# A ninth expert pair in a once-used buffer of its own, and GpSimd's transfers issued by SyncE

## What is computed

```python
n = rms_norm(h, g_mix)
proj = n @ w_in                       # z, xbc, dt, q, k, v, two gates
y_ssd = ssd_mixer(z, xbc, dt, ...) @ w_ssd_out
y_sb = stick_breaking_attention(q, k, v) @ w_sb_out
h = h + (gates[0] * y_ssd + gates[1] * y_sb) @ w_out
h = h + memory_cross_attention(rms_norm(h, g_xattn), rms_norm(mem, g_mem), w_xq, w_xkv, w_xo)
h = h + moe_ffn(rms_norm(h, g_moe), w_router, b_router, w_gu, b_gu, w_down, b_down)
return rms_norm(h, g_final)
```

## Time and profile before

| what | us |
|---|---|
| median of 3 runs | 1315.87 (1315.59 to 1319.79) |
| profiled execution, its own time | 1318.25 |
| its span in the profile | 1316.4 |
| PE busy | 1221.2 (93%) |
| DVE, ACT, POOL busy | 311.3, 230.5, 230.8 |

### The profile page before, as it was taken

How to read it: one execution, slowest core, us unless ns; L and a number is a source line. 1 busy time by engine, 2 the same in 40 slices (tenths; PEclk the granted TensorE clock), 3 DMA queues, 4 the chain that set the end, 5 groups by cost and what they waited for, 6 DMA issues and landing times.

```text
span 1316.4 us, 13854 instructions
## 1 busy us (share of the span) xinstructions
PE 1221.2 (93%) x5869; PEld 603.4 (46%) x5869; DVE 311.3 (24%) x452; ACT 230.5 (18%) x284; POOL 230.8 (18%) x205
## 2 busy tenths in 40 slices
PE   5999997898799999999999999999999999999996
PEld 5987776787643333333333333333333333333332
DVE  3526354314231112122111111211111111111111
ACT  4463674245100000000000000100000000000001
POOL 6776746776000000000000000000000000000000
PEclk9999998899879999999999999999999999999999
DMA  9543423454719999999999999999999999999994
GB/s 296 186 140 123 160 96 108 160 176 183 328 61 418 428 429 426 427 428 427 428 428 426 429 428 428 426 427 428 429 428 427 427 429 428 427 427 428 427 427 184
DMA packets 51498, 452.03 MB, mean 343 GB/s; under 512 B 4060, under 2 KB 4216, under 8 KB 26696
## 3 DMA queue, kind: packets, MB, share of 16 engines
q1 hardware_dynamic: 50680, 448.85, 82.8%
q0 software_dynamic: 752, 2.21, 0.6%
HBM read 450.00 MB, written 1.05 MB: 343 GB/s over the span
## 4 chain that ended last, share of the span: by engine, by line
PE 69%; DMA 24%; DVE 2%; issue 2%; ACT 1%; POOL 0%; POOLq 0%; SPq 0%; ACTq 0%; DVEq 0%
PE ps L920 23%; DMA ring<-in_w_gu 13%; PE ps L962 12%; PE ps L605 11%; DMA gates_xn<-in_w_gu 10%; PE ps L592 7%; PE ps L859 4%; PE ps L885 3%; PE ps L893 3%; PE ps L620 1%; PE ps L943 1%; PE ps L935 1%; PE ps L755 0%; PE ps L697 0%; DMA h<-in_x 0%
## 5 line engine op out<-in xcount | busy, mean ns | idle before, releaser
L385 POOL TENSOR_TENSOR w_parts<-ring,w_parts 128x512 fp32r<-128x512 f32 x160 | 214.1, 1371 | 84.8 <-ACT w_parts L1013 84.6
L920 PE MATMUL ps<-ring,nT 128*64 128x512 f32 x768 | 175.2, 604 | 17.8 <-DMA ring<-in_w_gu 17.8
L920 PE MATMUL ps<-ring,xs 128*64 128x512 f32 x768 | 175.1, 608 | 9.6 <-DMA ring<-in_w_gu 5.2
L480 POOL TENSOR_SCALAR ss<-ss 128x2 f32<-128x2 f32 (+2 forms) x7 | 1.3, 191 | 995.0 <-ACT junk L1003 975.0
L962 PE MATMUL ps<-ring,xbuf 128*64 128x512 f32 x768 | 171.4, 595 | 0.7 <-issue 0.7
L1209 ACT ACTIVATE xbuf<-xbuf 128x512 f32<-128x512 f32 x32 | 20.1, 630 | 780.1 <-DVE xbuf L1622 780.1
L1622 DVE TENSOR_SCALAR xbuf<-ps 128x512 f32<-128x512 f32 x32 | 22.1, 692 | 454.9 <-PE ps L920 454.9
L605 PE MATMUL ps<-w_parts,xT_hi 128*128 128x512 f32 x352 | 113.7, 404 | 8.9 <-issue 8.9
L920 PEld LDWEIGHTS ps<-ring,nT 128*64 128x64 f32 x768 | 54.3, 139 | 135.6 <-issue 101.6
L920 PEld LDWEIGHTS ps<-ring,xs 128*64 128x64 f32 x768 | 55.6, 140 | 125.7 <-issue 112.9
L962 PEld LDWEIGHTS ps<-ring,xbuf 128*64 128x64 f32 x768 | 53.4, 137 | 115.1 <-issue 115.1
(11 more groups left out here) (276 smaller groups left out, 1098.8 us busy)
## 6 DMA issues: line engine op xcount, KB each, us to landing
ring<-in_w_gu SPq DMA_DIRECT2D x96, 2048.0 KB, 30.1
ring<-in_w_down SPq DMA_DIRECT2D x47, 2048.0 KB, 35.1
kv_small<-in_w_gu SPq DMA_DIRECT2D x16, 2048.0 KB, 29.9
gates_xn<-in_w_gu SPq DMA_DIRECT2D x16, 2048.0 KB, 31.2
ring<-in_w_in SPq DMA_DIRECT2D x24, 1024.0 KB, 5.2
gates_xn<-in_w_down SPq DMA_DIRECT2D x8, 2048.0 KB, 35.2
kv_small<-in_w_down SPq DMA_DIRECT2D x8, 2048.0 KB, 33.4
ring<-in_w_ssd_out SPq DMA_DIRECT2D x4, 1024.0 KB, 5.0
```

The lines of the kernel that those rows point to most:

```text
L385: ops.tensor_tensor(w_lo[:, m % SPLIT, c], ring_slot(m)[:, c], w_hi[:, m % SPLIT, c], ALU.subtract).then_inc(lo_ready[name], 1)
L920: i = mm(ps[64 * half:64 * half + 64, 4 + q, :], xg[:, k, (j % GE) * SLOTS:(j % GE + 1) * SLOTS], w[:, q * FF + half * 512:q * FF + half * ...
```

## The change

Pair 8 goes into `spare`, with no wait of its own, right behind pair 7; `spare` is not used again. Pair 9 takes the buffer of pair 0, and so on: up to pair 16, pair m waits for pair m-9, from 17 on for the one that last held its buffer, m-8. Since buffers and pairs are offset by one from the second group on, the first eight experts differ from a loop's body, and PE does them as straight code ahead of a loop that now runs twice. All transfers of GpSimd are issued by SP between chunks.

```diff
-def pair_filled(m):
-
-    return 16 * (m // PAIRS + 1)
+def pair_filled(m, first):
+
+    if first and m <= PAIRS:
+        return 16
+    return 16 * ((m - 1 - PAIRS) // PAIRS + 2)
...
-        xbuf = sb("xbuf", [P, 3136])
+        xbuf = sb("xbuf", [P, 3072])
...
-        prow = sb("prow", [ROWS, P])
+        spare = sb("spare", [P, 2, CH])
...
-        w_dt = sb("w_dt", [P, KD, H_SSD])
...
+        w_dt = nc.alloc_sbuf_tensor_at("w_dt", [P, KD, H_SSD], F32, offset=aligned_of["xs"])
...
+        prow = xbuf[0:ROWS, 0:P]
...
-        def pair(m):
-
-            q = PAIR_ORDER[m % PAIRS]
-            return {KV_SMALL: kv_small, GATES_XN: gates_xn}[q][:, :, :] if q >= RING // 2 else ring[:, 2 * q:2 * q + 2, :]
+        def pair_at(m, first):
+
+            if first and m == PAIRS:
+                return None, spare[:, :, :]
+            n = m if first and m < PAIRS else (m - 1) % PAIRS
+            q = PAIR_ORDER[n]
+            return n, ({KV_SMALL: kv_small, GATES_XN: gates_xn}[q][:, :, :] if q >= RING // 2
+                       else ring[:, 2 * q:2 * q + 2, :])
...
+                if m == RING_SPLIT - 1:
+                    sp_.dma_start(w_dt[:], w_in[0, :, COL_DT:COL_Q].rearrange("(k p) n -> p k n", p=P)
+                                  ).then_inc(dtw_in, 16)
+                    for i, vec in enumerate((dt_bias, a_log, d_skip)):
+                        sp_.dma_start(head_rows[:, i, :], vec[0].partition_broadcast(P)).then_inc(dtw_in, 16)
+                if m == RING_SPLIT + 1:
+                    sp_.dma_start(wr[:].rearrange("p (c k) n -> p c k n", k=2),
+                                  w_router[0].rearrange("(c p k) n -> p c k n", p=P, k=2)).then_inc(late_in, 16)
+                    sp_.dma_start(gmoe[:].rearrange("p (c k) -> p c k", k=2),
+                                  g_moe[0].rearrange("(c p k) -> p c k", p=P, k=2)).then_inc(late_in, 16)
+                    sp_.dma_start(brt[:], b_router[0].partition_broadcast(P)).then_inc(late_in, 16)
+                if m == CHUNK_AT[(FIRST["gate"] + 3, 1)]:
+                    sp_.wait_ge(ydiag, 8)
+                    sp_.wait_ge(xw_ready, 1)
+                    sp_.dma_start(memx[:], mem[0].rearrange("(b p) d -> p b d", p=P)).then_inc(mem_in, 16)
+                if m == CHUNK_AT[(FIRST["xk"], 1)]:
+                    sp_.wait_ge(sb_o, 4)
+                    sp_.dma_start(bgu, b_gu[0]).then_inc(moe_in, 16)
+                    sp_.dma_start(bdn, b_down[0]).then_inc(moe_in, 16)
+                if m == CHUNK_AT[(FIRST["xq"], 0)]:
+                    sp_.wait_ge(chunk_used, products_done(FIRST["sb_out"] + 2))
+                    sp_.dma_start(gfin, g_final.partition_broadcast(P)).then_inc(gf_in, 16)
...
+                        q, w = pair_at(m, first)
+                        to_fill = spare_full if q is None else pair_full[q]
 
                         if first and m < PAIRS:
                             first_free(m)
-                        else:
-                            sp_.wait_ge(chunk_used, it * STEP_PR + (FRONT_CH + m - PAIRS + 1))
+                        elif q is not None:
+                            back = PAIRS + (first and m <= 2 * PAIRS)
+                            sp_.wait_ge(chunk_used, it * STEP_PR + (FRONT_CH + m - back + 1))
                         if c < GU_PR:
                             src = w_gu[0, bass.ds(g * BODY + j, 1), c * 2 * P:(c + 1) * 2 * P, :]
-                            sp_.dma_start(pair(m), src.rearrange("e (p k) n -> p (e k) n", p=P)
-                                          ).then_inc(pair_full[m % PAIRS], 16)
+                            sp_.dma_start(w, src.rearrange("e (p k) n -> p (e k) n", p=P)).then_inc(to_fill, 16)
                         else:
                             r = (c - GU_PR) * 4 * P
...
-            pool.dma_start(w_dt[:], w_in[0, :, COL_DT:COL_Q].rearrange("(k p) n -> p k n", p=P)).then_inc(dtw_in, 16)
-            for i, vec in enumerate((dt_bias, a_log, d_skip)):
-                pool.dma_start(head_rows[:, i, :], vec[0].partition_broadcast(P)).then_inc(dtw_in, 16)
...
-            pool.dma_start(wr[:].rearrange("p (c k) n -> p c k n", k=2),
-                           w_router[0].rearrange("(c p k) n -> p c k n", p=P, k=2)).then_inc(late_in, 16)
-            pool.dma_start(gmoe[:].rearrange("p (c k) -> p c k", k=2),
-                           g_moe[0].rearrange("(c p k) -> p c k", p=P, k=2)).then_inc(late_in, 16)
-            pool.dma_start(brt[:], b_router[0].partition_broadcast(P)).then_inc(late_in, 16)
-            for m in range(LO_DVE, 19):
-                low_part(pool, nc.gpsimd, "pool", m)
-
-            pool.wait_ge(ydiag, 8)
-            pool.wait_ge(xw_ready, 1)
-            pool.dma_start(memx[:], mem[0].rearrange("(b p) d -> p b d", p=P)).then_inc(mem_in, 16)
-            for m in range(19, 23):
+            for m in range(LO_DVE, 23):
...
-            for m in range(24, 26):
-                low_part(pool, nc.gpsimd, "pool", m)
-
-            pool.wait_ge(sb_o, 4)
-            pool.dma_start(bgu, b_gu[0]).then_inc(moe_in, 16)
-            pool.dma_start(bdn, b_down[0]).then_inc(moe_in, 16)
-            for m in range(26, 33):
-                low_part(pool, nc.gpsimd, "pool", m)
-            pool.wait_ge(chunk_used, products_done(FIRST["sb_out"] + 2))
-            pool.dma_start(gfin, g_final.partition_broadcast(P)).then_inc(gf_in, 16)
-            for m in range(33, 38):
+            for m in range(24, 38):
...
+            def pair_wait(it, m, first):
+
+                q, w = pair_at(m, first)
+                if q is None:
+                    pe.wait_ge(spare_full, pair_filled(m, first))
+                else:
+                    pe.wait_ge(pair_full[q], it * (16 * STEP_PR // PAIRS) + pair_filled(m, first))
+                return w
...
-            with pe.Fori(0, NIT - 1) as g:
+            experts(0, first=True)
+            with pe.Fori(1, NIT - 1) as g:
                 experts(g)
...
-    nc = bacc.Bacc("TRN2", target_bir_lowering=False, num_devices=1)
+    nc = bacc.Bacc("TRN2", target_bir_lowering=False, num_devices=1, dynamic_dma_scratch_size=1024)
```

More of the change, by code:

```diff
@@ L374, in build @@
         out_sem, out_ready = sem("out_sem"), sem("out_ready")
-        tail_full = sem("tail_full")
+        tail_full, spare_full = sem("tail_full"), sem("spare_full")
         block = ctx.enter_context(nc.Block())
@@ L448, in expert_pairs @@
                                 "e (p k) n -> p (e k) n", p=P)
-                            dst = pair(m).rearrange("p a (k n) -> p (a k) n", k=2)
+                            dst = w.rearrange("p a (k n) -> p (a k) n", k=2)
                             if last and m == STEP_PR - 1:
-                                sp_.dma_start(dst[:, 0:2, :], src[:, 0:2, :]).then_inc(pair_full[m % PAIRS], 16)
+                                sp_.dma_start(dst[:, 0:2, :], src[:, 0:2, :]).then_inc(to_fill, 16)
                                 sp_.dma_start(dst[:, 2:4, :], src[:, 2:4, :]).then_inc(tail_full, 16)
                             else:
-                                sp_.dma_start(dst, src).then_inc(pair_full[m % PAIRS], 16)
+                                sp_.dma_start(dst, src).then_inc(to_fill, 16)
             expert_pairs(0, 0, first=True)
@@ L625, in _ @@
             pe.wait_ge(consts, 9)
-            nc.tensor.transpose(ps[:, 3, 0:ROWS], prow[:], ident[0:ROWS, 0:ROWS]).then_inc(pt_done, 1)
+            nc.tensor.transpose(ps[:, 3, 0:ROWS], prow, ident[0:ROWS, 0:ROWS]).then_inc(pt_done, 1)
             transposes(TR_X, xn)
@@ L903, in residual, with experts @@
                    start=False, stop=False, skip_group_check=True)
-            def experts(it, last=False):
+            def pair_wait(it, m, first):
[5 more added lines that the diff above has]
+                return w
+            def experts(it, first=False, last=False):
                 for j in range(BODY):
@@ L915, in experts @@
                         if k % 2 == 0:
-                            pe.wait_ge(pair_full[m % PAIRS], it * (16 * STEP_PR // PAIRS) + pair_filled(m))
-                        w = pair(m)[:, k % 2, :]
+                            gu = pair_wait(it, m, first)
+                        w = gu[:, k % 2, :]
                         for q in range(2):
@@ L955, in experts @@
                         if k % 4 == 0:
-                            pe.wait_ge(pair_full[m % PAIRS], it * (16 * STEP_PR // PAIRS) + pair_filled(m))
+                            w = pair_wait(it, m, first).rearrange("p a (k n) -> p (a k) n", k=2)
                         if end and k == FF // P - 2:
                             pe.wait_ge(tail_full, 16)
-                        w = pair(m).rearrange("p a (k n) -> p (a k) n", k=2)
                         fh, c = k // 4, k % 4
```

## The result

The changed kernel takes 1309.34 us (median of 5 runs, 1307.68 to 1310.38); the kernel before took 1315.87 (1315.59 to 1319.79, also 5 runs). The medians lie 6.5 us apart. The ratio of the two kernels is 0.9936, with a 95% interval of 0.9915 to 0.9957, which is 8.4 us less (5.7 to 11.2). Forecast were 9.8 us less and 1306.1 us, in a range from 1303.1 to 1311.6. Over 15 runs of the changed kernel and 65 of the one before, made with the experiments, the medians lie 8.5 us apart. The profiled execution took 1310.38 us, 7.9 less than the one before; its span is 1308.6 us.

The account below looks back on a forecast made before the run. The DMA queue was taken to bound the expert stage, PE and chains between stages the front. 4.9 (ninth pair) + 4.4 (transfers) + 0.5 (clock) = 9.8 us; 1315.87 - 9.8 = 1306.1 us, range 1303.1 to 1311.6.

Parts of the forecast that it names:

- What bounds the kernel: Expert stage: the DMA queue alone sets the end, PE has 46.5 us to spare; PE and chains between stages set the front.
- The ninth pair: Expert weights' queue: pair 8 loads in the gap behind pair 7, one pair less later; 4.9 us, bounds 0 and 4.9.
- Rival 3: Expert weights' queue: a later hole opens, the ninth pair gives nothing, only the front's 4.9 us remain; 1311.0 us, chance 0.05.
- The transfers that leave GpSimd: First half of `xT_lo` near 208 us: DVE takes 2.19 us, PE starts 4.4 us earlier; bounds 1.1 and 5.3.
- the clock: Behind PE's pause at 207 us: a shorter pause means less time at half clock, 0.5 us; bounds 0 and 2.6.
- the front's gain: Ahead of the experts: 4.9 us, from 4.4 for the transfers leaving GpSimd and 0.5 for the clock.
- Rival 1: `xT_lo` near 208 us: POOL's whole row of subtractions holds DVE, transfers don't matter; gain 4.9 + 1.1, 1309.9 us, chance 0.15.
- Rival 2: Front: the timed runs have no such DVE stall, so only the ninth pair is left; 1311.0 us, chance 0.12.
- Rival 4: SP's queue behind chunk 4: small pieces land late and delay ACT's chunk 3; 5.7 us slower, 1321.6, chance 0.05.
- What costs nothing: Front: the other transfers moved from GpSimd to SP, between chunks, neither gain nor cost time; PE doesn't see `w_dt` land later.

Follow-up runs that it names:

- e1: The changed kernel with eight buffers, no ninth pair; all transfers stay on SP and the straight code stays: 1314.73 us, ratio 0.9955.
- e4: The kernel before with only the two bias transfers (`bgu`, `bdn`) moved from GpSimd to SP: 1313.28 us, ratio 0.9951.
- e3: The changed kernel without the ninth pair, the two bias transfers issued by GpSimd again, but behind low part 26: 1313.26 us, ratio 0.9955.
- e2: The changed kernel without the ninth pair, the two bias transfers issued by GpSimd again between low parts 25 and 26: 1317.66 us, ratio 0.9996.
- e5: The changed kernel itself, run a second time with nothing altered: 1309.82 us, ratio 0.9941.
- e6: The changed kernel with all nine buffers used in turn for four rounds (36 pairs), then eight: 1308.07 us, ratio 0.9927.
- e11: The kernel e6 (nine buffers in turn, no yields) run a second time: 1309.04 us, ratio 0.9917.
- e8: The changed kernel with `w_dt` and the three rows of head parameters issued behind chunk 6 instead of chunk 4: 1311.16 us, ratio 0.9939.
- e9: On top of e6, GpSimd holds low part 13 back until DVE has done its part: 1308.48 us, ratio 0.9919.
- e10: On top of e6, GpSimd holds low parts 26 and 38 back until DVE has done its part: 1307.31 us, ratio 0.9905.

## Why the prediction was right, and where it was off

**What bounds the kernel** held. PE comes to the last pair of `w_gu` and waits 1.25 us for it, as before; what shortened the queue's work or let it begin sooner came out at the end, and PE's straight code for the first eight experts, which e1 keeps, changed nothing (a stage of 902.47 us against 902.60).

**The ninth pair: predicted 4.9, measured 4.1 to 4.2 us.** The mechanism was right, but this sentence was wrong: "Every later pair is released by the same product as the pair one before it in the old order". It holds for pairs 9 to 16. Because the ninth buffer is used once, pair 17 and all behind it wait again for the product of the pair eight before, the same as before the change, while the queue has moved one pair ahead. It runs dry when pair 18 isn't yet allowed (432.56 us), since PE is just between `w_gu` and `w_down` of the second expert, where it finishes no product for some 10 us. The three windows from 430 to 436 us lack 107, 288 and 165 of 427 GB/s, which over 2 us each is 2.6 us of the queue.

Why the loss is 0.8 and not 2.6 us, the transfer records tell in part. I summed the bytes that the weights' queue had landed when PE could start the last pair of `w_gu`, and set them against the pairs up to that one, in order (182 pairs with eight buffers, 181 with nine). The surplus belongs to later pairs, which the 16 DMA engines had already moved in part while that pair was still unfinished. It is worth 5.3 us at 427 GB/s before (5.3 in e1, 5.2 in e4, 5.0 in e3, 4.6 in e2, whose stage is the shortest with eight buffers), 3.4 in the changed kernel (3.6 in e5), and 4.4 in e6 (4.3 in e11). So the sum is 4.9 - 2.6 + 1.9 = 4.2 us for the changed kernel, where 4.2 were measured (902.60 - 898.36), and 4.9 + 0.9 = 5.8 for e6, where 5.8 were. That is a balance of bytes and no cause. That e6 gains more than the one pair breaks my upper bound of 4.9: a pair less is not all that a ninth buffer changes. Why fewer bytes of later pairs run ahead of the last one is open.

Rival 3 had the right mechanism (a later hole in the queue) at too high a price (all 4.9 us). I set against it that the queue is full for 870 us, and a full queue in the old order says nothing about one that runs a pair ahead of its releases.

**The transfers that leave GpSimd: predicted 4.4, with 0.5 for the clock.** That two of the twelve matter is shown by e4, and that they do it by being issued just ahead of low part 26 by e2 and e3. The size of DVE's operation, 1.71 us in place of the 2.19 that I took, is right within 0.5 us, and PE's wait is 4.83 us shorter (7.68 to 2.85) for the 4.4. PE came back at 212.03 in the first profile and at 209.34 in the second, where I had 210.4. The 2.1 us by which the first is late are not made at this place: ACT starts the high part that precedes it at 206.35. Windows from 107 us, first of the changed kernel, then of the kernel before:

```profile
107.00:110.50 3.50, 3.44 (x5) 1.17 (x4) 3.50 (x4) 0.76 (x2) 0.62 (x1) 0.51 0.47 125
```

```profile
107.00:110.50 3.50, 2.95 (x10) 1.60 (x9) 3.50 (x5) 1.72 (x3) 0.61 (x1) 1.00 0.47 121
```

PE runs here at a granted clock of 0.51 (1.2 GHz), and before it did not, though it had waited for the same operations of DVE in both; two products at 108.2 us take 2.07 us on the chain where they took 1.12. That is 1.0 of the 2.1 us. In e5, the same kernel, this stretch is missing. It is not the only way to be late: e4 has none there either, and its high part starts at 206.27, since it had lost 1.3 us by the high part of chunk 3 (27.39 us for 26.09), with a half clock from 17.8 to 24.7 us. How much of the front's gain is left at the first product thus varies: over seven profiles without the stall and without a yield (changed, e1, e3 to e6, e11) it comes at 379.1 us in the mean, over the two with it (before, e2) at 382.1, which is 3.1 us. A steadier measure of the front is the time from the high part of chunk 26, just ahead of the stall, to that of chunk 41: 120.1 us before and 118.9 in e2, 114.1 to 115.1 in the eight profiles without the stall or a yield (changed, e1, e3 to e6, e8, e11). PE's shorter wait (4.83 us) is the greater part of that.

The clock's 0.5 us is not borne out. PE's 144 products behind the stall take 35.34 us before, with 5.2 us at a half clock in work, and 34.53 in the first profile of the changed kernel, with 3.4 us at half (a window from 212.9 to 216.3 shows 0.50), which looks like a gain of 0.8. But in e5, the same kernel, they take 35.22, with 4.9 us at half, and in e2, which has the whole stall, 34.45. So the length of the wait does not settle what the clock takes behind it, and that the sum comes out near 0.5 is luck.

The timed runs say more than the profiles. The three kernels with eight buffers and no stall (e1, e3, e4) have a median of 1313.8 us over 27 runs; the kernel before has 1318.1 over the 65 runs made beside all these, so the front's gain is 4.3 us for the 4.9 forecast. The changed kernel, 1309.55 over 15 runs, has 4.2 more, as much as the stage shows. Together that is 8.5 us for the 9.8 forecast, short by 0.7 at the ninth pair and by 0.6 in the front.

Part of the 4.3 us is how often an execution has little clock. Each of 60 of the runs before has its mean granted clock on record: 28 have 0.98 or more and a median of 1316.1 us, 27 have 0.975 or less and 1322.7. Of the 27 runs of e1, e3 and e4 13 have 0.98 or more, with 1313.1, and one has 0.975 or less. At like clock the front's gain is thus 3.0 us; the rest comes from executions at a low clock, which hardly occur in these three kernels. That the stall brings them about is not shown.

**Rival 1** (DVE held by the whole row of subtractions, and the transfers not the cause) fell with 1.71 us in the changed kernel, and e2 against e3 shows it at one place. The Trainium skill (SBUF — State Buffer, Who interferes with whom) has it that whichever instruction starts first keeps the port and, as an inference, that the making of descriptors doesn't hold up a `tensor_tensor`. In e2 the trace does not agree: VectorE's operation started first, during an issue, and was held for 6.67 us. In the changed kernel it agrees with the first half: the 1.71 us are the rest of the subtraction under way and the 1.2 us of the operation itself, and GpSimd's next subtraction, at 210.81 us, takes 2.27 us in place of some 1.25.

**Rival 2** (the timed runs have no such stall) fell as well. The profiled execution of e2 took 1315.42 us, among the fastest of that kernel, and has the stall. What its premise rested on, a median 2.4 us under the profile, is spread: the kernel before scatters from 1315.3 to 1324.9 us in these 65 runs, and of e2's ten runs four lie above 1322, while no run of e1, e3 or e4 lies above 1317.3. The forecast started from the 1315.87 of three runs, which sits at the low edge of that spread; with the 1318.1 of the 65 the forecast's 9.8 us would stand against 8.5.

**Rival 4** (small pieces in SP's queue) did not come: `w_dt_hi` starts at 21.36 us and ACT is at chunk 3 at 26.10. Its price was wrong too: "From 26.09 on every microsecond late is one of the whole". e8 makes ACT 6.55 us late and loses 1.3 us at most. There is waiting to make up at this place: in the changed kernel ACT stands 4.43 us for PE ahead of chunk 3 and GpSimd waits for ACT ahead of every low part, while in e8 GpSimd makes 24 subtractions from 34.68 to 64.79 us without a wait. Nor were the small pieces dear: the 1408 pieces of 64 bytes of the four transfers pass from 18.7 to 21.0 us and take 15.0 us in all, 0.9 for each of the 16 engines. The 81 GB/s of the earlier trace rows, on which I put that price, come from a window in which the three rows of head parameters, issued by GpSimd, take 17.8 of the 32 us of engine time (16 records of 512 bytes a row). From SP's queue the same rows are cheap.

**What costs nothing** did cost nothing: e4, which leaves ten of the twelve transfers on GpSimd, is as fast as e3, which leaves only the two biases there (1313.28 and 1313.26 us).

## What to carry to other kernels

Where a queue refills buffers as they are used, follow which use releases each fill at least two rounds on, and use a new buffer in turn with the others, not once: used once it gave 4.1 to 4.2 us, in turn 5.8. An operation that takes five times as long as its twins is worth more than any share on the page: look at what the other engines were starting when it started, not at what they were doing for most of its time. And a wait put in so that one engine yields to another pays only if the work held back isn't the next thing that is waited for (e9 against e10).

## What the runs showed that I had not expected

- A DVE subtraction of 128x1024 from two SBUF tensors that starts while GpSimd issues a transfer is held through all four of the subtractions that follow (6.54 us before, 6.67 us in e2), while one that starts with a GpSimd subtraction running takes 1.7 us, less than the 2.19 I had from the earlier trace rows, and 1.23 us with GpSimd waiting. Why the start decides so much is open.
- The two kernels with the stall scatter over more than 9 us (1315.3 to 1324.9, 1315.1 to 1324.5), the three with eight buffers and without it over 5.6 (1311.7 to 1317.2); but e8, without the stall, scatters over 8.9 (1307.4 to 1316.3). The scatter goes with the mean granted clock: before, all twenty executions above 1321 us whose clock is on record have 0.969 to 0.975, the 24 below 1317 have 0.980 to 0.984. No profile caught an execution above 1318.3, so where they lose the clock is open.
- The granted clock falls to one half for 3.4 to 13.7 us at a time, and partly at places that differ between two executions of the same kernel. At 107 us it costs 1.0 us, ahead of the first product of the experts 2.5 us.
- Up to 5.3 us' worth (2.3 MB, more than one pair) of later transfers is already in when an earlier one of the same queue is complete, and this changed with the number and use of the buffers (5.3, 4.4, 3.4 us) at the same 427 GB/s.
- An issue on SP behind large transfers that haven't landed can block SP: chunk 4 takes 2.43 us, `w_dt` 2.54 us and the first row of head parameters 5.21 us, where an issue of 2 MB in the expert stage takes 0.33. Here nothing stood behind them that was due.
